# An expert panel's two transfers: 64 partitions with 16 KB rows in place of 128 partitions with 8 KB rows

## What is computed

```python
D_MODEL, SEQ, N_EXPERTS, TOP_K, D_FF_EXPERT = 1024, 256, 8, 2, 3584

def moe_swiglu(h, w_router, w_gate_up, w_down):
    t = h.reshape(-1, D)
    logits = (t @ w_router).astype(F32)
    top_val, top_idx = lax.top_k(logits, TOP_K)
    top_w = jax.nn.softmax(top_val, axis=-1)
    combine = jnp.sum(jax.nn.one_hot(top_idx, N_EXPERTS, dtype=F32) * top_w[..., None], axis=1)
    out = jnp.zeros_like(t)
    for e in range(N_EXPERTS):
        gt, up = jnp.split(t @ w_gate_up[e], 2, axis=-1)
        y = (jax.nn.silu(gt) * up) @ w_down[e]
        out = out + combine[:, e:e + 1].astype(t.dtype) * y
    return out.reshape(B, S, D)
```

## Time and profile before

| | |
|---|---|
| median of 3 runs | 3510.34 us (3507.63 to 3511.9) |
| the profiled execution's own time | 3508.23 us |
| its span (first to last instruction) | 3506.1 us |
| mean granted TensorE clock | 0.928 of full speed |
| PE busy | 3089.0 us (88%) |
| DVE busy | 2047.3 us (58%) |
| ACT busy | 1526.7 us (44%) |
| read from device memory | 602.26 MB, 172 GB/s over the span |
| expert stage: first panel issued, last panel's second half of `w_lo` begun | 735.6 and 2107.7 us |

### The profile page before, as it was taken

The page is one execution under the profiler, slowest core; times in us unless marked ns, Lnnn a source line. Parts: engine busy times, 40 slices in busy tenths (PEclk is TensorE's granted clock), DMA queues, the critical chain, the costliest instruction groups (busy, mean ns, idle before and its releaser), DMA issues. The chain is left out here.

```text
span 3506.1 us, 41875 instructions
## 1 busy us (share of the span) xinstructions
PE 3089.0 (88%) x16917; PEld 2662.3 (76%) x16917; DVE 2047.3 (58%) x2209; ACT 1526.7 (44%) x1706; POOL 98.7 (3%) x111
## 2 busy tenths in 40 slices
PE   4979978679999999999999997988979696977897
PEld 4859876468888888878888887976777595975796
DVE  3447635545455455488898894533555555586644
ACT  3433333234434344367777773422334353422443
POOL 1000000000000000000000000000000000060000
PEclk8989998879999999999999998988989897988998
DMA  4427641035445444589999994423332242435042
GB/s 146 144 67 250 226 143 49 0 152 188 172 170 190 170 185 177 188 312 351 358 363 351 353 364 158 157 72 108 111 137 101 85 145 72 144 98 171 20 173 91
DMA packets 207396, 605.99 MB, mean 173 GB/s; under 512 B 20008, under 2 KB 78150, under 8 KB 163943
## 3 DMA queue, kind: packets, MB, share of 16 engines
q1 hardware_dynamic: 200890, 587.83, 46.4%
q0 software_dynamic: 4064, 12.75, 1.2%
q10 hardware_dynamic: 2253, 2.77, 0.2%
HBM read 602.26 MB, written 1.05 MB: 172 GB/s over the span
## 5 line engine op out<-in xcount | busy, mean ns | idle before, releaser
L1516 DVE TENSOR_TENSOR w_lo<-ring,w_hi 128x2048 fp32r<-128x2048 f32 x336 | 769.7, 2292 | 368.1 <-ACT w_hi L1446 363.2
L339 DVE TENSOR_TENSOR w_lo<-ring,w_hi 128x2048 fp32r<-128x2048 f32 (+2 forms) x228 | 473.7, 2080 | 598.4 <-ACT w_hi L330 597.9
L1446 ACT ACTIVATE w_hi<-ring 128x2048 fp32r<-128x2048 f32 x336 | 643.3, 1916 | 387.7 <-PE ps L1401 193.7
L330 ACT ACTIVATE w_hi<-ring 128x2048 fp32r<-128x2048 f32 (+2 forms) x228 | 396.4, 1739 | 773.3 <-PE ps L437 576.3
L437 PE MATMUL ps<-h_hi,w_hi 128*128 128x256 f32 x1608 | 469.1, 292 | 56.7 <-PEq L176 34.0
L437 PE MATMUL ps<-h_lo,w_hi 128*128 128x256 f32 x1608 | 465.4, 289 | 0.0
L437 PE MATMUL ps<-h_hi,w_lo 128*128 128x256 f32 x1608 | 465.0, 289 | 0.0
L437 PEld LDWEIGHTS ps<-h_hi,w_hi 128*128 128x128 f32 x1608 | 319.9, 199 | 63.1 <-issue 62.8
L437 PEld LDWEIGHTS ps<-h_lo,w_hi 128*128 128x128 f32 x1608 | 319.8, 199 | 0.2
L437 PEld LDWEIGHTS ps<-h_hi,w_lo 128*128 128x128 f32 x1608 | 319.4, 199 | 0.0
L1380 PE MATMUL ps<-w_hi,h_hi 128*128 128x512 f32 x672 | 267.5, 398 | 6.1 <-DVE w_lo L1516 6.1
(11 more groups left out here) (475 smaller groups left out, 5916.5 us busy)
## 6 DMA issues: line engine op xcount, KB each, us to landing
ring<-in_moe_w_gate_up SPq DMA_DIRECT2D x224, 1024.0 KB, 7.1
ring<-in_moe_w_down SPq DMA_DIRECT2D x112, 1024.0 KB, 6.9
ring<-in_w_in SPq DMA_DIRECT2D x54, 1024.0 KB, 6.4
ring<-in_w_in_even SPq DMA_DIRECT2D x28, 1024.0 KB, 6.3
ring<-in_dense_w_gate_up SPq DMA_DIRECT2D x22, 1024.0 KB, 7.8
ring<-in_w_in_odd SPq DMA_DIRECT2D x16, 1024.0 KB, 7.3
arena<-in_w_ada POOLq DMA_DIRECT2D x24, 512.0 KB, 4.8
ring<-in_w_out_even SPq DMA_DIRECT2D x12, 1024.0 KB, 7.3
```

What stands on the lines that cost most here:

```text
L330: k.nc.scalar.activation(self.part(k.w_hi, b, m), src, ACT.Copy).then_inc(k.hi_ready, 1)
L339: k.nc.vector.tensor_tensor(self.part(k.w_lo, b, m), src, self.part(k.w_hi, b, m).bitcast(F32), ALU.subtract).then_inc(k.lo_ready, 1)
L1446: nc.scalar.activation(high(g, h), raw(g, h), ACT.Copy).then_inc(k.hi_ready, 1)
L1516: nc.vector.tensor_tensor(low(g, h), raw(g, h), high(g, h).bitcast(F32), ALU.subtract).then_inc(k.lo_ready, 1)
```

## The change

Before, each of a panel's two transfers writes half of the slot's columns in all 128 partitions: 128 rows of 8 KB, which lie 16 KB apart in device memory. After, each writes all of the slot's columns in half of the partitions: 64 rows of 16 KB, which lie one behind the other in device memory. The first transfer fills partitions 0 to 63, the second partitions 64 to 127. Both still add 16 to the same semaphore, and nobody waits for the one alone. The number of transfers, their sizes in bytes, their places in SP's list and every wait are as before; the lists of PE, DVE, ACT and POOL are the same, row for row. Other weights' panels, loaded at L289, are not touched.

```diff
@@ -1293,9 +1293,9 @@
                     src = r.gate_up[:, ds(expert * GATE_PANELS + c, 1), :] if c < GATE_PANELS else \
                         r.down[:, ds(expert * DOWN_PANELS + (c - GATE_PANELS), 1), :]
                     for h in range(2):
-                        cols = slice(h * (SLOT // 2), (h + 1) * (SLOT // 2))
-                        sp.dma_start(k.ring[:, m.slot, cols].unsqueeze(1),
-                                     src[:, :, cols]).then_inc(k.panel_loaded[m.slot], 16)
+                        rows = slice(h * (P // 2), (h + 1) * (P // 2))
+                        sp.dma_start(k.ring[rows, m.slot, :].unsqueeze(1),
+                                     src[rows, :, :]).then_inc(k.panel_loaded[m.slot], 16)
```

## The result

| | before | after |
|---|---|---|
| median | 3508.99 us (4 runs) | 3881.01 us (4 runs) |
| lowest to highest | 3496.48 to 3511.9 | 3872.44 to 3881.79 |
| span of the profiled execution | 3506.1 | 3870.3 |
| mean granted clock | 0.928 | 0.902 |

The changed kernel takes 1.1059 times as long, with a 95% interval of 1.1043 to 1.1074. The medians lie 372 us apart; forecast were 399. The two profiled executions lie 364 us apart: the changed kernel's was the fastest of its four.

A forecast was written before the change was run, and what follows sets the result against it. PE was taken to bound the kernel, with transfers within 5% of it in the one-tile part. 3508.2 + 396 (one-tile part) + 2 (start) = 3906, about 3909 us as a median, 11.4% more; range 3560 to 4030.

The forecast's parts named there:

- The bound and its place: Expert stage: PE bounds everywhere; DMA engines busy 0.47 to 0.50 in two-tile part, 0.95 to 0.96 in one-tile part.
- the sum: Whole kernel: 3508.2 + 396 (one-tile part) + 2 (stage start) = 3906 us; as a median about 3909 us.
- The new price of a panel: Expert panels: loads into 64 partitions get 213 GB/s, half of 426, so 9.85 us a panel in place of 4.9.
- Two-tile part, 0: Two-tile part: no loss, 9.85 us being less than the 11.7 us between issues; DMA share rises to about 0.85.
- Start, +2 us: Start of the expert stage: first panel lands at 747.5, ACT began at 746.18; with 1 us more allowed, +2 us.
- The end of the part: End of one-tile part: last landing 2503.5, then 6.5 us ACT and DVE, 2.7 PE; last matmul 2512.7, +396 us.
- The ends of its ranges: Kernel time at half of the full rate: 3885 us (9.65 us a panel) to 4030; 11.1 us gave 4035; chance 0.58.
- (A) no change: One-tile part: 64 partitions load as fast as 128, 4.9 us a panel, kernel 3510 us; chance 0.17.
- (B) drift: One-tile part: engines out of step write both halves at once, 7.4 us a panel, kernel 3660 us; chance 0.16.
- (C) a clock that makes PE the bound: One-tile part: PE gaps halve the clock, 11.4 us a panel, kernel 4066 us; chance of worse than half rate 0.09.

The follow-up runs named there:

- e5: The change in the first 63 panels (two-tile part) only, the last 105 as in the kernel before: 3512 us, 1.0015 times the kernel before.
- e12: The change in the last 105 panels (one-tile part) only, the others as in the kernel before: 3876 us, 1.0993 times the kernel before.
- e8: Against the changed kernel, each 64-partition transfer with 16 KB rows takes every second partition: 3508 us, 0.9996 times the kernel before.
- e3: Against the changed kernel, four transfers a panel of 32 neighbouring partitions with 16 KB rows, in order: 3883 us, 1.1075 times the kernel before.
- e9: Against the changed kernel, four transfers of 32 partitions with 16 KB rows, the two halves in turn: 3773 us, 1.0756 times the kernel before.
- e2: Against the changed kernel, four transfers of 64 partitions with 8 KB rows, first half then second: 3864 us, 1.1022 times the kernel before.
- e10: Against the changed kernel, eight transfers of 64 partitions with 4 KB rows, the halves in turn: 3779 us, 1.0773 times the kernel before.

## Why the prediction was right

**The bound and its place.** Right. The windows had the one-tile part within 5% of a DMA bound and the two-tile part at half of it. e5 and e12 put 0.15% and 9.9% on the two. (The page of before has six slices at 9 tenths, not seven; the sum does not use it.)

**The new price of a panel.** Right in kind, and the term that was mis-sized: 9.85 us forecast between two landings, 9.56 measured. Over 100 panels that is 29 us, and the forecast was 28 us too high (3909 for 3881). Two errors stand in it against each other: the rate within one half is lower than half of 426 (205 GB/s, 10.2 us), and each change of halves gives some 0.35 us back. The reason given, a limit for each partition, was wrong: what is halved is the way into a half of the partitions. That both give the same number for this cut is luck. The same reason would have forecast 3909 us for e8, which took 3508, and some 5300 for e3, which took 3883. The Trainium skill's page SBUF — State Buffer, section "Door 1: The DMA port swizzle", gives 218 GB/s as the limit for 64 partitions and 196 as measured at 1 MiB. The sustained 215 to 229 GB/s lie by the first and a little above it, and the packets within one half, 205, between the two.

**Two-tile part, 0.** Right: 701.7 us after 701.6. The share rose to 0.80 and 0.84 (0.85 forecast). From 1080 to 1180 us the landings lie between 7.6 us, the panel's first transfer, and 12.1, its second; 12 was forecast for that one.

**Start, +2 us.** ACT waited 2.01 us for the first panel in the changed kernel's profile, and 1.63 us in e5's. Up to the one-tile part it came to 3.8 us in both, so some 2 us stand in no term of the sum.

**The end of the part.** The last matmul (L1401) ends at 2484.3 us, 367.7 us later than before, 396 forecast. Against the sum's 2512.7 the first landing is 0.1 us early, the 100 intervals give 29.1 us less, and what follows the last landing takes 10.1 us for 9.2.

**The ends of its ranges.** By the sum itself 9.65 us a panel gives 3889 us and not 3885, and 11.1 us gives 4035, just outside the stated 4030. Neither bears on the result.

**The rivals.** (A) no change: would have needed 357 GB/s; it had 217. (B) drift: would show only in the 6% by which the rate rises over the part (215 GB/s from 1550 to 1650 us, 229 from 2350 to 2450), and more in e9. (C) a clock that makes PE the bound: the granted clock was 0.85 to 0.88 in the one-tile part, so it fell in some gaps, but PE was idle for about a quarter of each window and never the bound, as argued.

## What to carry to other kernels

A panel that is loaded in two transfers should be cut by columns, or by every second partition, and never into partitions 0 to 63 and 64 to 127: each of those reached about half of the rate here, and two behind one another on the same queue do not make it whole. Here the price was hidden where the DMA engines had been busy for half of the time, and showed where they had been busy for 0.95 of it. So read the DMA share by stage before judging a change in a transfer's shape: the same edit cost 0.15% in 63 panels and 9.9% in 105. And take a price from what limits it: 426 GB/s over 128 partitions fitted two mechanisms with the same number, which only partitions chosen otherwise (32, or every second) told apart.

## What was not expected of the hardware

- The rate into one half is a little under half: 16 KB take an engine 1.28 us within one half (205 GB/s for 16 engines) and 0.61 us in e8 (429 GB/s).
- 32 neighbouring partitions of a half are as fast as its 64 (3883 and 3881 us).
- Every second partition is as fast as all 128, although a transfer names 64 partitions only (landing 7.2 us in the median, 7.1 before).
- Turning the order of two transfers in every second panel costs 31 us in itself (3912 against 3881).
- SP needs 0.47 us to issue a transfer of 64 rows of 16 KB, where one of 128 rows of 8 KB took 0.33. The length of the rows has no part in it: 64 rows of 8 KB (e2) or 4 KB (e10) took 0.47 us too, 32 rows of 16 KB (e3) 0.32. It is hidden here: SP waits for most of the stage.
